# Two value projections per head computed token-major, and the attention scores in column tiles, inside a one-core transformer kernel

## What is computed

```python
u = rms_norm(h, ln_mix_pre[l])
hq, hf, hi, hg, aq, ak, av = jnp.split(u @ w_in[l], split_at, axis=-1)
o_rec = hgrn2_mixer(hq, hf, hi, hg, lb_all[l], hgrn_norm[l])   # values: hi
o_att = dilated_attention_mixer(aq, ak, av)                    # values: av
mixed = jnp.concatenate([o_rec, o_att], axis=-1) @ w_out[l]
```

## Time and profile before

| | us |
|---|---|
| median of three runs | 1749.28 (1748.97 to 1749.44) |
| the profiled execution | 1749.28 |
| its span, first to last instruction | 1747.5 |
| TensorE busy, matmuls | 1737.8 (99%) |
| VectorE busy | 1238.5 (71%) |
| ScalarE busy | 939.4 (54%) |
| GpSimd busy | 627.4 (36%) |
| mean granted TensorE clock | 0.999 |

### The profile page before, as it was taken

One profiled execution on the slowest core, in us unless ns is written; L12 is line 12 of the kernel. 1 busy time (PEld: TensorE's weight loads), 2 busy tenths in 40 slices (PEclk: granted clock), 3 DMA queues, 4 the chain that ended last, 5 costly groups with the idle time before them and its releaser, 6 DMA issues.

```text
span 1747.5 us, 29776 instructions
## 1 busy us (share of the span) xinstructions
PE 1737.8 (99%) x10583; PEld 1520.5 (87%) x10583; DVE 1238.5 (71%) x1563; ACT 939.4 (54%) x1259; POOL 627.4 (36%) x629
## 2 busy tenths in 40 slices
PE   9999999999999999999999999999999999999998
PEld 8888888888888888888888888888888888888887
DVE  7877777765598777777777644445887578797754
ACT  6645555554466555555555443334655577675542
POOL 2854444557614333111111322122263166660032
PEclk9999999999999999999999999999999999999999
DMA  8444444437565555555555555556555555444453
GB/s 341 167 169 168 170 170 169 169 142 265 193 233 186 186 191 190 192 192 191 185 186 185 176 185 194 184 195 199 192 193 192 197 175 182 174 170 165 178 192 121
DMA packets 51357, 327.77 MB, mean 188 GB/s; under 512 B 5720, under 2 KB 6752, under 8 KB 18656
## 3 DMA queue, kind: packets, MB, share of 16 engines
q1 hardware_dynamic: 50144, 324.85, 53.0%
q10 hardware_dynamic: 1152, 2.11, 0.3%
HBM read 324.83 MB, written 2.11 MB: 187 GB/s over the span
## 4 chain that ended last, share of the span: by engine, by line
PE 94%; DVE 2%; issue 2%; POOL 1%; ACT 0%; DMA 0%; POOLq 0%; DVEq 0%; SPq 0%; ACTq 0%
PE ps L1978 56%; PE ps L1979 28%; PE ps_lev L2366 1%; PE ps_lev L2364 1%; PE ps_lev L2365 1%; PE ps_lev L1978 1%; DVE wlo L1081 1%; PE ps_t L2007 1%; POOL lev_in L1850 1%; PE ps_sc L2015 1%; DMA stage<-in_w_a 0%; PE ps_lev L2124 0%; PE ps_lev L1979 0%; PE bank_a L2020 0%; ACT whi L516 0%
## 5 line engine op out<-in xcount | busy, mean ns | idle before, releaser
L1978 PE MATMUL ps<-act_a,whi 128*128 128x512 f32 x2928 | 1026.0, 394 | 0.0
L1081 DVE TENSOR_TENSOR wlo<-stage,whi 128x2048 fp32r<-128x2048 f32 (+1 forms) x314 | 693.8, 2210 | 246.0 <-ACT whi L516 241.5
L1979 PE MATMUL ps<-act_a,wlo 128*128 128x256 f32 x2928 | 818.6, 280 | 0.0
L1978 PEld LDWEIGHTS ps<-act_a,whi 128*128 128x128 f32 x2928 | 549.8, 188 | 121.5 <-issue 2.0
L516 ACT ACTIVATE whi<-stage 128x2048 fp32r<-128x2048 f32 (+1 forms) x314 | 566.1, 1803 | 133.1 <-DMA stage<-in_w_down 105.9
L1979 PEld LDWEIGHTS ps<-act_a,wlo 128*128 128x128 f32 x2928 | 550.0, 188 | 0.6
L1978 PE MATMUL ps<-big,whi 128*128 128x512 f32 x1456 | 506.5, 392 | 0.3 <-DVE pg_x L1093 0.3
L1979 PE MATMUL ps<-big,wlo 128*128 128x256 f32 x1456 | 407.0, 280 | 0.0
L523 ACT ACTIVATE small<-ps 128x256 f32<-128x256 f32 x227 | 86.9, 383 | 492.8 <-PE ps L1979 492.7
L1978 PEld LDWEIGHTS ps<-big,whi 128*128 128x128 f32 x1456 | 273.3, 188 | 60.7 <-DVE pg_x L1093 0.6
L1979 PEld LDWEIGHTS ps<-big,wlo 128*128 128x128 f32 x1456 | 273.4, 188 | 0.1
(11 more groups left out here) (426 smaller groups left out, 1541.0 us busy)
## 6 DMA issues: line engine op xcount, KB each, us to landing
stage<-in_w_a SPq DMA_DIRECT2D x165, 1024.0 KB, 4.7
stage<-in_w_b SPq DMA_DIRECT2D x86, 1024.0 KB, 4.8
stage<-in_w_down SPq DMA_DIRECT2D x64, 704.0 KB, 4.0
three<-in_w_three SPq DMA_DIRECT2D x7, 384.0 KB, 9.5
mem_raw<-in_memT SPq DMA_DIRECT2D x1, 2048.0 KB, 10.8
mem_again<-in_memT SPq DMA_DIRECT2D x1, 2048.0 KB, 9.0
x_in<-in_x_turned ACTq DMA_DIRECT2D x7, 256.0 KB, 9.1
x_in<-in_xT SPq DMA_DIRECT2D x3, 512.0 KB, 5.7
```

The lines of the kernel that those rows point to most:

```text
L1081: dve.tensor_tensor(wlo[:, slot, part], stage[:, slot, part], whi[:, slot, part].bitcast(F32), ALU.subtract).then_inc(w_lo, 1)
L1978: pe.matmul(dst, whi[:, slot, c * P:(c + 1) * P], act, start=start, stop=False)
L1979: return pe.matmul(dst[:, T:2 * T], wlo[:, slot, c * P:(c + 1) * P], act[:, 0:T], start=False, stop=stop)
```

## The change

For heads 1 to 7 the two value blocks become a pair of blocks in which each of 16 feature tiles has 128 columns of `hi` and 128 of `av` side by side. `token_values` multiplies them with the tokens stationary and the weights moving, three matmuls of 256 columns for each half of the tokens and each feature tile, 48 in a block, into the two halves of the bank `ps_t`. ScalarE copies both halves with the token's norm as its scale (`values_kept`), for which head 0 turns `rstd` once (`scales_turned`) and keeps two columns of it (`x_col`). The value blocks' evacuations, sums, scalings and turns fall away. The order of a head becomes hf, hq, aq, ak, pair, pair, hg, so that queries and keys come one and two blocks sooner; `attention_out` and `early_levels` move behind the second pair block, and the scores follow them, for heads 1 to 7 as twelve matmuls in column tiles of 32 queries that leave out masked key ranges (`turned_scores`). The queries are no longer stored reversed; the second half of the output is reversed instead, which makes one copy on ScalarE and one difference on VectorE into two each. ScalarE and VectorE get new orders: the norm of the recurrence's output comes before the values are kept, `attention_max` before the late levels, and in head 1 `recurrence_weighted(0)` stands five cells into block 3 instead of before it.

```diff
             def attention_out(n):
                 wait(act, "att_out", n + 1)
-                act.activation(xs_mix[:, bass.ds(HEADS + n, 1), 0:T], ps_b.unsqueeze(1), ACT.Copy).then_inc(s("att_hi"), 1)
+                for half, order in ((slice(0, P), slice(0, P)), (slice(P, T), slice(T - 1, P - 1, -1))):
+                    act.activation(xs_mix[:, bass.ds(HEADS + n, 1), half], ps_b[:, order].unsqueeze(1), ACT.Copy).then_inc(s("att_hi"), 1)
...
+            def values_kept(i, u):
+                act.wait_ge(w_used, u + 5 + 1)
+                wait(act, "hg_out", i)
+                wait(act, "att_out", i)
+                for t in range(2):
+                    act.activation(values[:, t, :, :], ps_t[:, t * T:(t + 1) * T].rearrange("p (a b) -> p a b", a=2), ACT.Copy,
+                                   scale=x_col[:, t:t + 1]).then_inc(s("values_kept"), 1)
...
(ScalarE, heads 2 to 7)
-                evac(u + 3, 1 - behind)
+                evac(u + 3, 1 - behind, blocks=3)
                 hi(start, i, 8, 6)
-                evac(u + 4, behind)
+                inverse_root(var[:, :], (s("var_ready"), before + 1), s("o_norm"))
                 hi(start, i, 8, 7)
+                recurrence_out(before)
+                values_kept(i, u)
                 attention_out(before)
-                turned(vtok, "i_turned", "vtok_ready", i)
-                evac(u + 5, 1 - behind)
                 hi(start, i, 8, 8)
-                inverse_root(var[:, :], (s("var_ready"), before + 1), s("o_norm"))
+                attention_exp(i)
                 if not memory:
                     cross(i)
-                attention_exp(i)
-                recurrence_out(before)
                 evac(u + 6, behind)
...
(VectorE, heads 2 to 7)
-                scaled(u + 2, behind, iT[:, :], "i_ready")
-                add(u + 3, 1 - behind)
+                queries_scaled(u + 2, behind)
+                add(u + 3, 1 - behind, blocks=3)
                 lo(start, i, 8, 6)
-                queries_scaled(u + 3, 1 - behind)
-                add(u + 4, behind)
+                scaled(u + 3, 1 - behind, akT[:, :], "ak_ready")
+                recurrence_variance(before)
                 lo(start, i, 8, 7)
-                scaled(u + 4, behind, akT[:, :], "ak_ready")
-                recurrence_variance(before)
+                recurrence_normed(before)
                 place_levels(i, range(4))
                 attention_split(before)
-                add(u + 5, 1 - behind)
                 lo(start, i, 8, 8)
-                scaled(u + 5, 1 - behind, avT[:, :], "av_ready")
+                attention_max(i)
                 if not memory:
                     place_levels(i, range(4, LEVELS))
-                attention_max(i)
-                recurrence_normed(before)
...
(TensorE)
+            def turned_scores(q, k):
+
+                for t in range(2):
+                    for part in range(4):
+                        pe.matmul(ps_sc[part_rows(part, 4), t * P:t * P + (P if t else (part + 1) * P // 4)],
+                                  q[:, part_rows(4 * t + part, 4)], k[:, 0:P if t else (part + 1) * P // 4], start=True, stop=True)
+                for part in range(4):
+                    after = P + part * P // 4
+                    ins = pe.matmul(ps_sc[part_rows(part, 4), P + after:3 * P], q[:, part_rows(4 + part, 4)], k[:, after:T], start=True, stop=True)
+                return ins
...
+            def token_values(start, i, n):
+
+                if n == 0:
+                    wait(pe, "pT_ready", i)
+                slot = (start + 4 + n) % NS
+                pe.wait_ge(w_lo, i * 8 + (start + 4 + n + 1))
+                for c in range(KT // 2):
+                    k, cell = n * KT // 2 + c, slice(c * T, (c + 1) * T)
+                    for t in range(2):
+                        half = ps_t[:, t * T:(t + 1) * T]
+                        x_hi, x_lo = act_a[:, k, t * P:(t + 1) * P], act_a[:, k, T + t * P:T + (t + 1) * P]
+                        pe.matmul(half, x_hi, whi[:, slot, cell], start=k == 0 and t == 0, stop=False)
+                        pe.matmul(half, x_hi, wlo[:, slot, cell], start=False, stop=False)
+                        ins = pe.matmul(half, x_lo, whi[:, slot, cell], start=False, stop=k == KT - 1 and t == 1)
+                ins.then_inc(w_used, 1)
...
(head 1)
-                recurrence_weighted(0)
-                whole(start, 1, 8, 3, u + 3, 0, act_a)
+                await_block(start, 1, 8, 3, u + 3)
+                cells((start + 3) % NS, 0, act_a, range(5), closes=False)
+                recurrence_weighted(0)
+                cells((start + 3) % NS, 0, act_a, range(5, KT), opens=False).then_inc(w_used, 1)
+                token_values(start, 1, 0)
                 pe.wait_ge(*event("ones_rounded"))
                 recurrence_summed(0)
-                whole(start, 1, 8, 4, u + 4, 1, act_a)
-                value_turned(1)
-                whole(start, 1, 8, 5, u + 5, 0, act_a)
+                token_values(start, 1, 1)
+                early_levels(1)
                 attention_scores(1)
-                early_levels(1)
                 last_block(start, 1, u, 1)
-                attention_value_turned(1)
...
(heads 2 to 7)
-                whole(start, i, 8, 4, u + 4, behind, act_a)
+                token_values(start, i, 0)
+                token_values(start, i, 1)
                 attention_out(before)
-                value_turned(i)
                 early_levels(i)
-                whole(start, i, 8, 5, u + 5, 1 - behind, act_a)
                 attention_scores(i)
                 if memory:
                     whole(start, i, 8, 6, u + 6, behind, act_a)
                     levels(i, range(4, LEVELS + 1))
                 else:
                     last_block(start, i, u, behind)
-                attention_value_turned(i)
```

More of the change, by code:

```diff
@@ L152, in build @@
         eps = sb("eps", [P, 1])
+        x_col = sb("x_col", [P, 2])
         conv_at = at[0]
@@ L516, in hi, with evac @@
                 act.activation(whi[:, slot, 0:cells * P], stage[:, slot, 0:cells * P], ACT.Copy).then_inc(w_hi, 1)
-            def evac(u, b, ahead=0, bank=None):
+            def evac(u, b, ahead=0, bank=None, blocks=1):
                 act.wait_ge(w_used, u + ahead + 1)
                 act.wait_ge(out_free, u + 1)
-                act.activation(small[:, b, :], (ps[:, b, :] if bank is None else bank)[:, T:2 * T], ACT.Copy).then_inc(small_ready, 1)
+                act.activation(small[:, b, :], (ps[:, b, :] if bank is None else bank)[:, T:2 * T], ACT.Copy).then_inc(small_ready, blocks)
             def inverse_root(t, waits, done, tables=True):
@@ L631, in first_head @@
                 hi(G_MIX, 0, 8, 8)
-                turned(vtok, "i_turned", "vtok_ready", 0)
+                act.wait_ge(*event("x_turned"))
+                turned(vtok, "i_turned")
+                act.activation(x_col[:, :], ps_t[:, T:2 * T:P], ACT.Copy).then_inc(event("x_col")[0], 1)
                 evac(U_MIX + 6, 0)
@@ L658, in second_head @@
                 mem_hi(range(12, KT))
-                evac(u + 3, 0)
+                evac(u + 3, 0, blocks=3)
                 hi(start, 1, 8, 6)
-                evac(u + 4, 1)
                 hi(start, 1, 8, 7)
                 inverse_root(var[:, :], (s("var_ready"), 1), s("o_norm"))
-                turned(vtok, "i_turned", "vtok_ready", 1)
-                evac(u + 5, 0)
+                act.wait_ge(*event("x_col"))
+                values_kept(1, u)
                 hi(start, 1, 8, 8)
@@ L2031, in attention_turned @@
                 wait(pe, "p_ready", 2 * n + 2)
-                wait(pe, "avtok_ready", n + 1)
+                wait(pe, "values_kept", 2 * n + 2)
                 for c in range(3):
@@ L2072, in levels, with value_turned, scales_turned @@
                         ins.then_inc(s("lev_ready"), 1)
-            def value_turned(i):
-                wait(pe, "i_ready", i + 1)
+            def value_turned():
+                pe.wait_ge(s("i_ready"), 1)
                 turn(ps_t[:, 0:P], iT[:, 0:P], None, 0)
                 turn(ps_t[:, P:T], iT[:, P:T], "i_turned")
+            def scales_turned():
+                pe.wait_ge(*event("x_norm"))
+                turn(ps_t[:, T:T + P], rstd[:, 0:P], None, 0)
+                turn(ps_t[:, T + P:], rstd[:, P:T], "summed")
+            def token_values(start, i, n):
[12 more added lines that the diff above has]
+                ins.then_inc(w_used, 1)
             def early_levels(i):
@@ L2085, in attention_scores, with attention_value_turned @@
             def attention_scores(i):
-                wait(pe, "aq_ready", 2 * i + 2)
+                wait(pe, "aq_ready", i + 1)
                 wait(pe, "ak_ready", i + 1)
                 wait(pe, "att_max", i)
-                masked_scores(aqT, akT).then_inc(s("sc_ready"), 1)
-            def attention_value_turned(i):
-                wait(pe, "av_ready", i + 1)
```

(15 more changed lines are left out.)

65 lines of the change are left out of this document (32 added, 33 removed).

## The result

| | us, median | runs |
|---|---|---|
| before | 1749.13 | 4 (1748.97 to 1749.44) |
| changed | 1773.06 | 4 (1772.22 to 1774.16) |

The ratio is 1.0137 with a 95% interval of 1.0125 to 1.0150. I forecast 1747.9, no change. The span grew from 1747.5 to 1771.8 us, 24.3 us, at the same granted clock (0.999).

The account below looks back on a forecast made before the run. TensorE was taken as the bound, its matmuls recorded over 99% of the span. Savings of 1.4 us took the span from 1747.5 to 1746.1, with 1.78 around it 1747.9; range 1745.1 to 1751.0.

Parts of the forecast that it names:

- the sum: Whole kernel: 1.44 + 0.21 + 0.21 - 0.3 - 0.2 = 1.4 us saved from the span of 1747.5, giving 1746.1.
- B: Token-major value blocks less dense from switching bank halves after every three matmuls; decides from 7.5 ns each (5.0 us); chance 0.10.
- Head 1: TensorE's 1.45 us stop goes, but it stands about 1.9 us before `ps_cross` for GpSimd; 0.21 us kept.
- A loop head: Heads 2 to 5: TensorE reaches `ps_cross` 0.20 us sooner, within the spare 0.53; 0.36 us kept each, 1.44 in all.
- the pair: Two value blocks of 48 matmuls, 5.63 us each against 5.55, cost 0.16 us more in a head.
- the scores: Scores in column tiles take 0.50 to 0.53 us instead of 0.66, saving 0.15; bounds no gain and 0.35.
- Head 6: The 0.20 us saved ahead of `ps_cross` goes into waiting for GpSimd, a stop of about 0.4; 0.21 us kept.
- Head 7: Late levels placed behind `attention_max` delay TensorE: saving of the turns gone and 0.3 us lost; bounds -0.2 and +1.5.
- The last output: After the mixers, a copy and a difference each become two, on one path: 0.2 us lost, bounds 0 and 0.5.
- A: GpSimd doesn't hold TensorE in heads 1, 6 and 7, a `lo` less in its chain: 2.6 us saved, 1745.2; chance 0.15.
- C: New wait on ScalarE or VectorE, in the loop or from head 6 to 7, takes gain back: 1749 to 1750; chance 0.12.
- D: Additional weight loads in the value blocks show: 224 at 0.188 us each, 42 us, 1790; chance 0.02.

Follow-up runs that it names:

- old addresses: The changed kernel with `x_col` put into unused room of `dummy`'s slot, so `act_a` and `big` lie where they did in the kernel before: 1750.01 us, ratio 1.0005.
- 128 bytes further: The changed kernel with 96 bytes of padding behind `x_col`, so `act_a` and `big` lie 128 bytes beyond their place in the kernel before: 1748.14 us, ratio 0.9995.
- 96 / 96: The kernel before with 96 unused bytes before the masks, so `act_a` lies 96 bytes further from both `whi` and `wlo`: 1754.31 us.

## Why the prediction was wrong, point by point

**The step that failed** is the sum. "From the span of 1747.5 that is 1746.1" takes the span of before and changes it by what the mixers do, so it prices every cell outside them by the earlier trace rows, where cells follow at 347 ns. I costed `x_col` as two transposes and a small copy and called it hidden; as an allocation it made 4272 cells 6.4 ns longer. Summed from start to start, old addresses against the kernel of the diff, the plain cells are 27.3 us longer; the 672 token-major matmuls are 1.5 shorter, the 288 other matmuls of 512 columns whose moving operand is a weight tile 1.2, the levels with the stop of head 1 0.5, all else 0.4. That leaves 23.7, and with the 0.6 by which the old addresses are longer than before it is the 24.3 of the span. None of the rivals was this one. B came nearest in kind, a pace that no row shows, but for 672 matmuls and by their pattern. B's bound of 7.5 ns was also never near: 0.5 to 2.7 ns were measured.

**The mechanisms**, on the changed kernel at the old addresses and 128 bytes further. A stretch runs from one `recurrence_weighted` to the next; in the kernel before these start at 101.35 (head 1), 297.00 (head 5), 340.67 (head 6) and 378.77 (head 7), and with 128 bytes of padding within 0.09 us of that. The last output ends at the first late cell. Of the +1.13 behind it 0.71 is the stop for the late weights; the other 0.4 I can't place.

| stretch | forecast | old addresses | 128 further |
|---|---|---|---|
| up to head 1 | -0.21 | -0.49 | -0.86 |
| heads 2 to 5 | -1.44 | -0.29 | -0.92 |
| head 6 | -0.21 | -0.38 | -0.51 |
| head 7 | +0.3 | +0.53 | +0.21 |
| last output | +0.2 | +0.10 | +0.09 |
| from there to the end | 0 | +1.13 | +0.69 |
| span | -1.4 | +0.6 | -1.3 |

- **Head 1.** The stop of 1.45 us is gone, and TensorE stands in front of `ps_cross` until GpSimd is through, 1.00 us at the old addresses:

```profile
93.65 0.46 POOL L1854 TENSOR_TENSOR lev_in<-kk,sfx 128x128 f32<-128x128 f32 x1
...
94.16 0.42 PE L2081 MATMUL bank_a<-lev_in 128*32 128x128 f32 x8 [1.00 <-POOL lev_in L1854]
```

  The chain ends at 94.11, where I had 94.4 and the kernel before 94.38; the saving of 1.65 us ahead of it came to 0.27. Right in kind; of the 1.9 us of standing that I forecast 0.9 are missing, 0.27 because the chain ended sooner, 0.26 in the token blocks, and the rest I can't place.
- **A loop head** takes 48.84 us, 48.68 at 128 further; forecast 48.55, before 48.91. The terms that were off are the pair (+0.42 at 120.0 ns, forecast +0.16, and +0.26 at 118.3) and the scores (-0.11 instead of -0.15). In the changed kernel as it is in the diff a head is 49.21: 96 cells times 6.6 ns are 0.63 us more, and the pair is 0.21 shorter.
- **Head 6** showed no stop where I forecast 0.4, and kept more than forecast.
- **Head 7.** A stop before `recurrence_weighted(7)` ended by VectorE was forecast at 0.3 and measured at 0.62 (0.52 in the kernel of the diff). 128 bytes further it does not appear, and TensorE stands 0.21 us in front of `ps_cross` instead.
- **The last output** costs 0.10 us, forecast 0.2. Behind it the late weights cost 0.71 us that no term had: I looked for what waits in the mixers and let the transfers be ("keep number and size"), though all of them would be asked for at other times.
- **Rivals.** A did not come: the chain of head 1 ended at 94.11 against 94.38, where a `lo` less would have taken some 2 us off it. C came in part: 0.62 us of standing in head 7, of which the sum had 0.3, and 0.71 behind the mixers, where C did not look. D did not show: 96 weight loads beside 96 matmuls in 11.3 us.

Had `x_col` lain inside a slot that was already there, the forecast of 1747.9 would have met 1750.0 and, 128 bytes further, 1748.1, all of them no change. That would have been luck in good part: at the old addresses the span grows by 0.6 us where 1.4 were to be saved, and the -1.3 of the last column is made of other terms than the forecast and compares two placements; against the kernel before with the same 128 bytes (1748.51) the change is worth 0.4 us, which can't be told from nothing.

## What to carry to other kernels

A tile added in front of large ones is part of the change: look at what its slot moves, and compare the start-to-start distance of an unchanged product far from the edit before anything else. If that differs, give the changed kernel the old addresses and the old kernel the new ones; the two runs split layout from edit. And where a forecast sums the gains of a stage, ask of the next stage's transfers whether they come sooner as well.

## What the hardware showed that I had not expected

- The pace of back-to-back matmuls depends on the distance in SBUF between moving and stationary tiles. 512 columns took 228.4 to 234.9 ns, 256 columns 116.2 to 120.4, for placements in steps of 32 bytes, at a granted clock of 0.999 or 1.0 throughout; over the program 1748 to 1775 us for the same instructions. The slower pace is there with no other engine and no transfer at work.
- At one placement both paces can come: with 96 / 96, 346.7 ns for 2355 cells and 353.3 for 381 later ones.
- The best distance for one product is not the best for another: that of before gave plain cells 346.7 ns and token-major matmuls 120.0, that of the changed kernel 353.3 and 117.8.
- A burst of weight transfers that was asked for 1.3 us sooner had its first block usable 1.2 us later.
